# Layer 0 of a two-layer decoder trunk: both groups of TensorE transposes moved within the attention's slot, next to the value products and to the slot's end

## The reference

```python
# layer 0, cut to what matters (SEQ 1024, D_MODEL 1024, 8 heads, head size 2 x 64, blocks of 128 queries)
u = rms_norm(h, a_norm_g) * (1 + scale) + shift            # shift, scale, gate: silu(c) @ a_ada_w + a_ada_b
q, k, v, z = jnp.split(u @ a_w_in, 4, axis=-1)
q = rms_norm(q.reshape(bsz, seq, 2 * A_HEADS, 64), a_q_norm_g)
k = rms_norm(k.reshape(bsz, seq, 2 * A_HEADS, 64), a_k_norm_g)
s = einsum('bqhd,bkhd->bhqk', q_block, k) * scale - sub_slopes * dist     # causal, ALiBi
p = softmax(s).reshape(bsz, A_HEADS, 2, 128, seq)
o = einsum('bhqk,bkhe->bqhe', p[:, :, 0] - lam * p[:, :, 1], v)           # the difference of two softmaxes
o = rms_norm(o, a_subln_g) * (1 - lambda_init) * silu(z)
h = h + gate * (o @ a_w_out)
# then shared keys and values from h, and layer 1: sliding-window attention with sinks; not touched here
```

## Time and profile before

| what | us |
|---|---|
| median of 3 runs | 1368.37 (1365.18 to 1370.67) |
| the profiled execution | 1369.13, its span 1367.3 |
| TensorE busy | 1180.5 (86% of the span) |
| VectorE busy | 854.5 (62%) |
| ScalarE busy | 697.8 (51%) |
| GpSimd busy | 234.1 (17%) |

### The profile page before, as it was taken

One profiled execution on the slowest core, in us unless ns is written; L12 is line 12 of the kernel. 1 busy time (PEld: TensorE's weight loads), 2 busy tenths in 40 slices (PEclk: granted clock), 3 DMA queues, 4 the chain that ended last, 5 costly groups with the idle time before them and its releaser, 6 DMA issues.

```text
span 1367.3 us, 22306 instructions
## 1 busy us (share of the span) xinstructions
PE 1180.5 (86%) x6192; PEld 933.1 (68%) x6192; DVE 854.5 (62%) x2644; ACT 697.8 (51%) x2161; POOL 234.1 (17%) x354
## 2 busy tenths in 40 slices
PE   0469899998989899898976997769999898995998
PEld 0357576675757677675754886668888787885886
DVE  6665666666566666666655323985887878776221
ACT  0655455554555555455543102975766766674100
POOL 1201212112121211212101112111111212110122
PEclk9989999999999999999986998879999999997999
DMA  8341131312223131222203334210020110103332
GB/s 299 113 140 62 50 98 41 112 55 62 94 63 94 45 98 55 87 70 71 85 27 116 131 138 169 78 47 16 12 78 13 47 42 28 62 28 109 116 125 86
DMA packets 53226, 111.42 MB, mean 81 GB/s; under 512 B 5904, under 2 KB 19216, under 8 KB 52112
## 3 DMA queue, kind: packets, MB, share of 16 engines
q1 hardware_dynamic: 53136, 110.51, 24.7%
HBM read 93.71 MB, written 16.78 MB: 81 GB/s over the span
## 4 chain that ended last, share of the span: by engine, by line
PE 69%; DVE 13%; issue 8%; ACT 6%; DMA 2%; POOL 1%; DVEq 0%; POOLq 0%; SPq 0%; ACTq 0%; PEldq 0%
PE ps_p L591 12%; PE ps_p L593 11%; PE ps_p L592 11%; PE ps_s L671 5%; PE ps_o L706 3%; PE ps_t L730 3%; PE ps_p L814 2%; PE ps_p L815 2%; PE ps_p L816 2%; PE ps_o L816 2%; PE ps_o L814 2%; PE ps_o L815 2%; PE ps_t L791 2%; ACT e L951 2%; DMA stage<-ada_w 2%
## 5 line engine op out<-in xcount | busy, mean ns | idle before, releaser
L591 PE MATMUL ps_p<-w_hi,u_hi 128*128 128x512 f32 x768 | 332.9, 434 | 14.6 <-DVE w_lo L1164 14.1
L593 PE MATMUL ps_p<-w_hi,u_lo 128*128 128x512 f32 x768 | 304.1, 396 | 0.0
L592 PE MATMUL ps_p<-w_lo,u_hi 128*128 128x512 f32 x768 | 302.7, 394 | 0.0
L591 PEld LDWEIGHTS ps_p<-w_hi,u_hi 128*128 128x128 f32 x768 | 146.0, 190 | 76.0 <-ACT ez L982 19.2
L593 PEld LDWEIGHTS ps_p<-w_hi,u_lo 128*128 128x128 f32 x768 | 145.3, 189 | 33.7
L592 PEld LDWEIGHTS ps_p<-w_lo,u_hi 128*128 128x128 f32 x768 | 146.9, 191 | 18.4
L951 ACT ACTIVATE e<-e,negm 128x256 f32<-128x256 f32 (+7 forms) x128 | 98.3, 769 | 115.3 <-DVE negm L1297 114.6
L1319 DVE TENSOR_REDUCE ssum<-sq 128x4 f32<-128x256 f32 x64 | 26.9, 420 | 133.0 <-ACT sq L977 133.0
L1017 ACT ACTIVATE pT<-ps_t 128x512 f32<-128x512 f32 (+2 forms) x96 | 43.6, 489 | 122.2 <-PE ps_t L730 122.2
L671 PE MATMUL ps_s<-kTa,qTa 64*128 64x512 f32 (+3 forms) x384 | 91.3, 553 | 8.2 <-DVE negm L1297 5.3
L469 POOL TENSOR_SCALAR ez<-ez 128x128 f32<-128x128 f32 x64 | 22.5, 351 | 436.6 <-ACT ez L982 436.6
(11 more groups left out here) (185 smaller groups left out, 2623.7 us busy)
## 6 DMA issues: line engine op xcount, KB each, us to landing
adabuf<-ada_w SPq DMA_DIRECT2D x64, 384.0 KB, 3.2
raw<-w_a SPq DMA_DIRECT2D x80, 256.0 KB, 3.4
raw<-w_b SPq DMA_DIRECT2D x48, 256.0 KB, 3.1
e<-ada_w SPq DMA_DIRECT2D x4, 1024.0 KB, 4.8
stage<-ada_w SPq DMA_DIRECT2D x4, 1024.0 KB, 4.8
e<-x SPq DMA_DIRECT2D x8, 512.0 KB, 3.4
oa_scratch<-ob SPq DMA_DIRECT2D x64, 64.0 KB, 1.6
e<-oa_scratch SPq DMA_DIRECT2D x8, 512.0 KB, 4.5
```

What stands on the lines that cost most here:

```text
L591: pe.matmul(o, u_hi[:, c, t], w_hi[:, c, :], start=(c == 0), stop=False)
L592: pe.matmul(o, u_hi[:, c, t], w_lo[:, c, :], start=False, stop=False)
L593: mm = pe.matmul(o, u_lo[:, c, t], w_hi[:, c, :], start=False, stop=(c == KD - 1))
```

## The change

In each slot of layer 0's attention TensorE's queue is reordered. The query/key transposes follow the value products directly (in slot 0 with the six small matmuls between), and chunk 3 of the projection follows them. The probability transposes follow chunk 7, and the next slot's first scores follow them directly. The instructions, their waits and their semaphores are the same; only chunk 3 and chunk 7 change places with the two groups of transposes. The new order is: scores part 0, chunks 0 to 2, scores part 1, value products, query/key transposes, chunks 3 to 7, probability transposes. The wait for `S.proj` behind the last tile's chunk 7 moves with chunk 7.

```diff
--- before.py
+++ after.py
@@ -713,7 +713,6 @@
                                 mm = pe.matmul(ps_o[:, i4 % 2, P + j:P + j + 1], ada_acc[:, j * P:(j + 1) * P], ones[:, :],
                                                start=True, stop=True)
                             mm.then_inc(ada_mm, 1)
-                    part_of_projection(range(3, 4))
                     if live(2):
 
                         pe.wait_ge(S.qn, n2 + 1)
@@ -722,14 +721,13 @@
                         for k in range(2):
                             mm = pe.transpose(ps_o[:, (i2 + 1) % 2, (2 + k) * P:(3 + k) * P], qn[:, k * P:(k + 1) * P], ident[:, :])
                         mm.then_inc(S.tr, 1)
-                    part_of_projection(range(4, 7))
+                    part_of_projection(range(3, KD))
                     if live(3):
 
                         pe.wait_ge(S.comb, n3 + 1)
                         for j in range(i3 + 1):
                             mm = pe.transpose(ps_t[:, j * P:(j + 1) * P], e0[:, i3 % 2, j * P:(j + 1) * P], ident[:, :])
                         mm.then_inc(S.pt, 1)
-                    part_of_projection(range(7, KD))
                 pipeline(pe, 8, units, 5, slot)
```

## The result

| what | before | after |
|---|---|---|
| median of 5 executions each, us | 1370.67 (1365.18 to 1372.61) | 1378.48 (1377.89 to 1380.91) |
| after / before | | 1.0068, 95% interval 1.0044 to 1.0092 |
| the profiled execution, its span | 1369.13, 1367.3 | 1379.04, 1377.2 |
| TensorE busy | 1180.5 | 1186.5 |

The account below looks back on a forecast made before the run. TensorE was taken to bound slot 3 to slot 0 and VectorE's chain slot 1. Slot terms of +1.68 us a unit made 13.4 over eight, +0.3 for start and edges: 1368.4 + 13.7 = 1382 us, range 1373 to 1391.

Parts of the forecast that it names:

- What bounds each slot: Layer 0's attention: TensorE bounds slot 3 to slot 0; VectorE sets slot 1's length, so slot 1 changes by 0.
- The new waits: Query/key transposes would wait for a late `ob`: slot 3 0.74 us, slot 4 0.49, slot 5 0.45, slot 6 0.42.
- A: The forecast's time anchor in a slot: the start of ScalarE's first copy `pT<-ps_t`, after the last probability transpose.
- The other terms: Per unit: slot 7 -0.14 us, slot 0 +0.29 (TensorE's wait for its own projection), slot 1 0, slot 2 -0.57.
- The joint: Probability transposes directly followed by the next scores: 0.11 us and a gap of 0.06 to 0.10, taken as 0.10.
- rival (c): The clock falls more often, six more falls where TensorE is the bound: 9.8 us, 1392 us; chance 0.10.
- 3 us less than now: The clock rival's other side: a fall behind the `w_lo` wait would lie in slot 1's slack and cost nothing.
- one more chunk before the very first probability transpose: At the start, one more projection chunk runs ahead of the first probability transpose: +0.69 us, once.
- (a): The holes are filled: 16 comb waits each take one more chunk, 11.0 us, giving 1357 us; chance 0.06.
- (b): The new waits in slots 3 to 6 don't cost, as `ob` moves along with the scores: 1366 us; chance 0.11.
- (d): In slots 4 to 6 `ob` doesn't gain from the earlier `sq`: 10 us, 1392 us; chance 0.05.
- The marks in the profile: Signs expected after: 35 to 39 `ob` waits, about 28 us; comb waits under 10; slots 3, 4, 2 at 9.0, 7.5, 11.1.

Follow-up runs that it names:

- e4: The changed kernel with the wait for `S.proj` and the release of the weights moved behind slot 0's probability transposes: 1376.49 us, ratio to before 1.0058.
- e9: The kernel before with slot 1's TensorE holes filled by small matmuls against a tile of zeros: 1366.71 us, ratio to before 0.9979.
- e10: The changed kernel with slot 1's TensorE holes filled by small matmuls against a tile of zeros: 1377.85 us, ratio to before 1.0062.
- e3: The changed kernel with slots 3 to 6's query/key transposes written to free `ps_t`, waiting for `qn` but not `ob`: 1369.91 us, ratio to before 0.9999.
- e6: The changed kernel with ScalarE's three reads of the new projection (`sq` first) ahead of the probability transposes' copy: 1363.62 us, ratio to before 0.9953.
- e8: e7 with chunk 3 back ahead of the query/key transposes: 1353.91 us, ratio to before 0.9885.
- e2: The kernel before with only chunk 7 moved ahead of the probability transposes; chunk 3 stays: 1365.38 us, ratio to before 0.9972.
- e5: e2 with the wait for the unit's last projection behind slot 0's probability transposes: 1362.06 us, ratio to before 0.9944.
- e7: e6 with the wait for the unit's last projection behind slot 0's probability transposes: 1360.10 us, ratio to before 0.9931.

## Why the prediction was right, and where its size was off

**What bounds each slot: right.** Slots 3 to 6 were TensorE's and pay for a late `ob`; slot 1 is a chain of the other engines and kept its length (15.88 for 15.91). Chunks 3 and 7 filled a hole there whose end didn't move.

**The new waits: right to 0.05 us.** Slot 3: `ob` was forecast to end at A + 4.88 and the transposes to start at A + 5.03; after has 420.55 + 0.34 - 416.01 = 4.88 and 421.03 - 416.01 = 5.02. Slot 4: forecast `sq` at A + 0.18, `ob` at A + 3.29, transposes at A + 3.44; after has 0.17, 3.27 and 3.41. The lengths are +0.73, +0.49 and +0.45 for 0.74, 0.49 and 0.45. Slot 6 was mis-sized: +0.37 for 0.42.

**The other terms.** Slot 0 +0.32 for 0.29, and e4 shows that it is the wait for `S.proj`; slot 2 -0.58 for -0.57; slot 7 -0.23 for -0.14, where the 0.09 has no explanation from a run. A unit: +1.52 for +1.68.

**The joint.** From the single probability transpose to the scores are 0.20 us in the kernel after (424.72 and 424.92), so 0.11 and a gap of 0.09, for which the forecast took 0.10. TensorE's weight loads there, kernel after:

```profile
424.49 0.14 PEld L729 LDWEIGHTS ps_t<-ident,e 128*128 128x128 f32 x1
424.92 0.30 PEld L671 LDWEIGHTS ps_s<-kTa,qTa 64*128 64x128 f32 x4 [0.29 <-issue]
```

The scores' load starts with the scores and not ahead of them. The Trainium skill, "TensorE: Matmul & The Clock Gate", Part 3, "The mechanism", has a weight load overlap matmuls under way only where their row groups differ. The scores' 64 rows lie within the transposes' 128, and for this joint the trace agrees. It doesn't for the transpose's own load: that one has 128 rows as well and starts 0.23 us ahead of its matmul (424.49 and 424.72), under a chunk's matmul of 128 rows. The same section also has a load pulled ahead when it goes to the background weight buffer; which loads go there, no row here tells.

**The term that was mis-sized: the clock.** The sum priced the falls at nothing and kept them for rival (c), as a loss with six more falls, and, in one sentence, for the other side, "3 us less than now". That sentence is what happened. In the profiled executions the granted clock fell more often (five units instead of two), and it cost less, since the fall moved with the hole from the comb wait to the `w_lo` wait, into slack. The totals of e9 and e10 point that way: without falls the kernels are 11.1 us apart, with them 9.3, a difference within the noise. The loops show it: 632.6 - 621.0 = 11.6 us without falls, 632.4 - 623.6 = 8.8 with them, and the two falls of the kernel before are 2.6 of that. The forecast's own share for the loop was 13.4 - 0.74 - 0.36 + 0.71 = 13.0. So of the 4.4 us between 13.7 and 9.3, some 2 to 3 are the clock, 1.4 (13.0 less 11.6) the slots 6, 7 and the drain's first part, which shrank by 0.7 with the change (12.94 and 12.25 in e9 and e10); the +0.69 for one more chunk before the very first probability transpose can't be seen in the totals.

**The rivals.** (a) and (b) needed `ob` to move along with the scores, and it didn't; that a kernel without its wait gets 9.4 us back (e3) excludes both. Rival (a) had one more condition: that slot 1's hole would shrink. It did in e6 to e8 alone, where its chain starts earlier. (c) is out: more falls, but all in slot 1 and none in slots 3 to 6, where the transposes now stand beside the waits. (d) is out: `ob` of slot 4 ends 0.54 earlier after A than before, and `sq` starts 0.53 earlier (3.27 for 3.81; 0.17 for 0.70).

**The marks in the profile.** 36 waits for `ob` came as forecast (35 to 39), but with 14.8 us and not 28. Two things were missed. The view's idle time is up to 0.2 us smaller than what a slot loses, as the record of the pipelined matmul ahead covers the first part: slot 3 shows 0.56 and is 0.73 longer, slot 6 shows 0.21 and is 0.37 longer. And slot 1's share is 1.8 only where the clock had stayed up; behind a fall the chunks ahead of the transposes take the time and 0.22 to 0.42 is left. The comb waits are 9.4 (under 10), the `w_lo` wait 2.49 (about 2.5), the lengths of slots 3, 4 and 2 9.01, 7.52 and 11.11 (9.0, 7.5 and 11.1).

**What stays open.** The loops of single profiled executions and the totals by the ratio differ by up to 3.5 us (e2: -7.3 and -3.8; e6: -9.2 and -6.4; e5: -9.8 and -7.7; e9: -2.6 and -2.9). The clock in the drain differs from kernel to kernel, and where the rest goes wasn't tested.

## What to carry to other kernels

Moving an engine's filler work ahead of its waits pays only where the slot's end hangs on that engine; list the slots, find the one link that ends each, and check for every instruction moved forward whether its producer moves forward too. Here one half of the edit alone was worth -3.8 us and the other alone +1.0, but both together +9.3, since they drew on one slack: halves that are each harmless have to be priced together. With the first half left out, the release of the weights late and the first link of the late chain (`sq`) moved first, the same idea is 1.15% faster than the kernel before (e8). A hole that is moved takes its fall of the clock along, so look at what stands behind it.

## What the runs showed of the hardware

**A fall costs what stands behind it.** The granted clock fell to 1.2 GHz for stretches of 3.4 us (0.57 as the mean of 4.00 us is 4.00 x 0.43 x 2) around the end of holes of 2.1 to 2.8 us in slot 1, in some units and not in others of the same kernel, and in none of e2, whose holes before `w_lo` are 2.5. The price was 1.5 us behind the comb wait (before), 0.4 to 0.7 behind the `ob` wait of e7 (15.34 to 15.62 for 14.97), and nothing behind the `w_lo` wait (after) or the `ob` wait of e8, where slack was left. The Trainium skill, "TensorE: Matmul & The Clock Gate", Part 1, "HAM oscillation", reckons the price of a throttled stretch as half its length; an estimate by that rule is 1.7 us for 3.4. The kernel before agrees with its 1.5, the kernel after doesn't with its 0.0, since its matmuls there weren't on the path.

**The mean clock of an execution.** Over 29 executions of the kernel before, a mean clock lower by 0.001 goes with 0.8 us more (1362.5 us at 0.967, 1374.8 at 0.958); over 11 of e2 there is no relation (1365.38 at 0.952, 1365.35 at 0.962). The two belong together in one kernel and not in the other, so the mean clock of a span says little without the places of the falls.

**Wake-up times.** In each slot in which the query/key transposes wait for `ob` last they start 0.15 us behind its end (421.03 for 420.55 + 0.34 in the kernel after); where they wait for `qn` alone (e3), 0.06.
